# Two transformer blocks on one core: where the norm sums are added, one root for two norms, and where table loads, modulation products and row starts lie

## The reference

```python
def rms_norm(x, gain):                 # _rmsnorm of the first block is the same
    y = x * rsqrt(mean(x * x, axis=-1) + 1e-6)
    return y * gain

def first_block(x, ...):
    x = x + moba(rms_norm(x, norm_mix), w_qkv, w_o)        # 16 heads, causal softmax
    u = causal_dwconv(rms_norm(x, norm_ffn) @ w_up, ...)   # 3 taps, 2 x 2816 columns
    x = x + (silu(gate) * up) @ w_down                     # gate, up: halves of u
    return rms_norm(x, norm_final)

def second_block(x, c, ...):
    sh1, sc1, ga1, sh2, sc2, ga2, sh3, sc3, ga3 = split(silu(c) @ w_mod + b_mod, 9)
    h = rms_norm(x, g_ffn1) * (1 + sc1) + sh1
    x = x + 0.5 * (1 + ga1) * swiglu(h, w1_gate, w1_up, w1_down)
    h = rms_norm(x, g_mix) * (1 + sc2) + sh2
    x = x + (1 + ga2) * hybrid_mixer(h, ...)   # 8 stick-breaking and 8 forgetting heads
    h = rms_norm(x, g_ffn2) * (1 + sc3) + sh3
    return x + 0.5 * (1 + ga3) * swiglu(h, w2_gate, w2_up, w2_down)
```

## Time and profile before

| | us |
|---|---|
| median of 3 runs | 902.32 |
| lowest and highest | 896.45, 907.48 |
| the profiled execution | 906.59 |
| its span, first to last instruction | 904.9 |
| PE busy | 874.3 |
| DVE busy | 668.9 |
| ACT busy | 484.6 |
| POOL busy | 57.4 |

### The profile page before, as it was taken

The page is one execution under the profiler, slowest core; times in us unless marked ns, Lnnn a source line. Parts: engine busy times, 40 slices in busy tenths (PEclk is TensorE's granted clock), DMA queues, the critical chain, the costliest instruction groups (busy, mean ns, idle before and its releaser), DMA issues.

```text
span 904.9 us, 17152 instructions
## 1 busy us (share of the span) xinstructions
PE 874.3 (97%) x6920; PEld 834.2 (92%) x6920; DVE 668.9 (74%) x1396; ACT 484.6 (54%) x1008; POOL 57.4 (6%) x99
## 2 busy tenths in 40 slices
PE   6999998999999998999999998999999999999998
PEld 5888887999999997999999998878878999999998
DVE  6676657989888997998889986555643898877551
ACT  6644434777666465555555455534533665555440
POOL 4000002000000131000000026000000100000000
PEclk9999999999999999999999999979979999999999
DMA  9765356665655997767679996133004577555640
GB/s 291 251 196 179 102 190 219 209 206 192 210 187 162 337 340 278 236 231 247 227 238 317 320 343 189 47 94 95 34 13 140 186 252 240 185 187 175 204 157 25
DMA packets 151071, 179.47 MB, mean 198 GB/s; under 512 B 5712, under 2 KB 141136, under 8 KB 150992
## 3 DMA queue, kind: packets, MB, share of 16 engines
q1 hardware_dynamic: 149536, 177.65, 59.2%
q10 hardware_dynamic: 432, 0.68, 0.2%
q0 software_dynamic: 1024, 0.03, 0.1%
HBM read 177.27 MB, written 1.05 MB: 197 GB/s over the span
## 4 chain that ended last, share of the span: by engine, by line
PE 83%; DVE 10%; ACT 4%; issue 1%; DMA 1%; POOL 0%; SPq 0%; DVEq 0%; POOLq 0%
PE bank L1149 24%; PE bank L1150 24%; PE bank L1151 24%; DVE wlo L834 4%; DVE mring L905 3%; PE bank L1190 3%; PE bank L1237 1%; PE bank L1202 1%; PE bank L1194 1%; PE bank L1181 1%; PE bank L1239 1%; PE bank L1238 1%; DMA raw<-in_moba_w_qkv 1%; PE bank L1193 1%; ACT Ahi L653 1%
## 5 line engine op out<-in xcount | busy, mean ns | idle before, releaser
L1149 PE MATMUL bank<-Ahi,whi 128*128 128x258 f32 (+2 forms) x1448 | 419.8, 290 | 17.5 <-DVE wlo L834 9.0
L1150 PE MATMUL bank<-Alo,whi 128*128 128x258 f32 (+2 forms) x1448 | 411.7, 284 | 0.0
L1151 PE MATMUL bank<-Ahi,wlo 128*128 128x258 f32 (+2 forms) x1448 | 411.4, 284 | 0.0
L834 DVE TENSOR_TENSOR wlo<-raw,whi 128x512 fp32r<-128x512 f32 x528 | 352.0, 705 | 47.3 <-ACT whi L633 46.2
L633 ACT ACTIVATE whi<-raw 128x512 fp32r<-128x512 f32 x528 | 302.6, 620 | 92.6 <-PE bank L1151 77.9
L1149 PEld LDWEIGHTS bank<-Ahi,whi 128*128 128x128 f32 (+1 forms) x1448 | 277.4, 192 | 22.1 <-issue 12.0
L1150 PEld LDWEIGHTS bank<-Alo,whi 128*128 128x128 f32 (+1 forms) x1448 | 277.7, 192 | 1.1 <-issue 1.0
L1151 PEld LDWEIGHTS bank<-Ahi,wlo 128*128 128x128 f32 (+1 forms) x1448 | 276.9, 191 | 0.0
L1149 PE MATMUL bank<-Hhi,whi 128*128 128x256 f32 x528 | 147.5, 279 | 0.0
L1150 PE MATMUL bank<-Hlo,whi 128*128 128x256 f32 x528 | 147.5, 279 | 0.0
L1151 PE MATMUL bank<-Hhi,wlo 128*128 128x256 f32 x528 | 147.5, 279 | 0.0
(11 more groups left out here) (142 smaller groups left out, 797.9 us busy)
## 6 DMA issues: line engine op xcount, KB each, us to landing
mring<-in_w_mod SPq DMA_DIRECT2D x72, 512.0 KB, 6.2
raw<-in_ffn_w_up SPq DMA_DIRECT2D x22, 1024.0 KB, 5.1
raw<-in_w_gate SPq DMA_DIRECT2D x22, 1024.0 KB, 5.2
raw<-in_w_up SPq DMA_DIRECT2D x22, 1024.0 KB, 5.3
raw<-in_w_down SPq DMA_DIRECT2D x16, 1024.0 KB, 5.7
raw<-in_w_in SPq DMA_DIRECT2D x12, 1024.0 KB, 5.5
raw<-in_moba_w_qkv SPq DMA_DIRECT2D x11, 1024.0 KB, 6.7
raw<-in_ffn_w_down SPq DMA_DIRECT2D x8, 1024.0 KB, 5.8
```

Source lines behind the costliest of these rows:

```text
L834: dve.tensor_tensor(lo, raw[:, i % RAW, k0:k1, 0:width], hi.bitcast(F32), ALU.subtract).then_inc(s_wlo, 1)
L1149: pe.matmul(o, hi, xh, start=kg == 0, stop=False)
L1150: pe.matmul(o, hi, xl, start=False, stop=False)
L1151: ins = pe.matmul(o, lo, xh, start=False, stop=last and kt == nk - 1)
```

## The change

1. **Row pitch.** Ahi and Alo become flat buffers. `tiles_of` cuts them in rows of 258 floats for up2, qkv3 and up4, and in rows of 256 (1024 bytes) for qkv1 and up1.
2. **Norm sums.** ACT squares two tiles in one instruction of 512 elements: the first pair straight into `acc`, now 2 x 2 x 256, later pairs into `sq`, one pair long. DVE adds the pair to `acc` in one instruction of 512. POOL adds nothing. TensorE sums two halves of `acc` for each norm, so two fp32 matmuls where there was one, with 1/1024 in the matrix in place of a scale on ACT.
3. **One root for two norms.** With m1 the mean of x^2 and m2 that of (g x)^2, both norms together scale by 1/sqrt(m2 + eps (m1 + eps)). The second squares of up2 are taken with `fcol` = sqrt(g^2 + eps), computed once early in qkv1 (`norm_columns`, on DVE and ACT), so one Ln with bias eps^2 and one Exp give the common factor; norm_final's own factor follows with another pair. The DVE products are gone.
4. **Table loads.** `exp_ln` is called at the first squares of a norm, and `silu`, now a load of its own, right behind the root of up1, up2 and up4.
5. **Modulation products.** Still 72, at other slabs.
6. **A one-column matmul** at the first k tile of each down phase, fp32, into a column of the norm bank that nobody reads.
7. `spread_f` waits for the last chunk of down2 before it fills FA and FB, which share their place with Hhi and Hlo. `lnb` and `fcol` move ahead of Hhi.

```diff
 MOD_STEPS = {
-    "qkv1": ..., "o1": lambda i: 1 + int(i == 16), "up1": lambda i: int(i == 30),
-    "down1": lambda i: 2 - i % 2, "up2": lambda i: int(i > 54) * (i % 2 + int(i % 16 == 8)), "down2": lambda i: 2 - i % 2,
+    "qkv1": ..., "o1": lambda i: 1 + int(i == 12) - int(i == 17), "up1": lambda i: int(i == 30),
+    "down1": lambda i: 2 * int(i < 47), "up2": lambda i: int(i > 56) * (i % 2 + int(i % 8 == 0)),
+    "down2": lambda i: 2 * int(i < 85),
...
+        def tiles_of(flat, ph):
+            row = SA if ph in SHIFTED else S
+            return flat[:, 0:KD * row].rearrange("p (k c) -> p k c", c=row)
...
             def spread_f():
+                last = plan.first_of["qkv3"] - 1
+                pool.wait_ge(s_chunk, plan.chunk_done[last, slabs[last][4] // 2 - 1])
...
+            def squares(ph, q):
+                if q == 0:
+                    exp_ln()
...
+                for j in range(2 if ph == "up2" else 1):
+                    if q == 0:
+                        need.wait_ge(s_sums, NORMS.index(ph))
+                        o = acc[:, j, :, :]
+                    else:
+                        need.wait_ge(s_acc, acc_index["up1", 2, 0] if ph == "up1" and q == 3 else acc_index[ph, q, j] - 1)
+                        o = sq[:, :, :]
...
+                    elif j == 0:
+                        act.activation(o, XT[:, 2 * q:2 * q + 2, :], ACT.Square).then_inc(s_sq, 1)
...
+            def root(o, src, e):
+                need.wait_ge(s_root, ln[0])
+                act.activation(lnb[:, :], src, ACT.Ln, bias=epsc[:, e:e + 1]).then_inc(s_ln, 1)
+                ln[0] += 1
+                need.wait_ge(s_ln, ln[0])
+                act.activation(o, lnb[:, :], ACT.Exp, scale=-0.5).then_inc(s_root, 1)
+
+            def norm(ph):
...
+                if ph == "up2":
+                    root(Rr[:, 0, :], b[:, S:2 * S], 1)
+                    root(Rr[:, 1, :], b[:, 0:S], 0)
                 else:
+                    root(Rr[:, 0, :], b[:, 0:S], 0)
+                if ph in ("up1", "up2", "up4"):
+                    silu()
...
+            def add_squares(ph, q):
+                if q == 0 or (ph == "up1" and q == 3):
                     return
+                for j in range(2 if ph == "up2" else 1):
+                    need.wait_ge(s_sq, sq_index[ph, q, j])
+                    need.wait_ge(s_acc, acc_index[ph, q, j] - 1)
+                    dve.tensor_tensor(acc[:, j, :, :], acc[:, j, :, :], sq[:, :, :], ALU.add).then_inc(s_acc, 1)
...
             def multiply(i, kt):
...
+                if tag == "down" and i == plan.first_of[ph] and kt == 0:
+                    pe.matmul(banks[NORM_BANK][:, 511:512], meanf[:, :], meanf[:, 0:1], start=True, stop=True)
```

More of the change, by code:

```diff
@@ L159, in lay @@
                 lower()
-                for m in (n - 1, n):
-                    st.put("sq", "qkv1", m, 0)
+                st.put("sq", "qkv1", n // 2)
         offer(1)
@@ L279, in evict @@
                     to = NEXT_NORM[ph]
-                    for n in (c0 // P, c0 // P + 1):
-                        if to != "up1":
+                    if to != "up1":
+                        for n in (c0 // P, c0 // P + 1):
                             st.put("ain", to, n)
-                        for j in range(2 if to == "up2" else 1):
-                            st.put("sq", to, n, j)
+                    st.put("sq", to, c0 // C)
         done = 0
@@ L378, in build_program @@
         XT = sb("XT", [P, KD, S])
[L379 to L380 removed]
+        Ahi_flat = sb("Ahi", [P, KD * SA], F32R)
+        Alo_flat = sb("Alo", [P, KD * SA], F32R)
         with ExitStack() as scope:
@@ L411, in build_program @@
         bcol = sb("bcol", [P, 4])
-        epsc = sb("epsc", [P, 1])
+        epsc = sb("epsc", [P, 2])
+        lnb = sb("lnb", [P, S])
+        fcol = sb("fcol", [P, 8])
         rs = sb("rs", [P, 4, 4])
@@ L460, in build_program @@
         stick = {n: k + 1 for k, n in enumerate(m for m, h in enumerate(heads) if h[0] == "sb")}
[L461 to L464, removed]
+        sq_parts = [(s[1], s[2], j) for s in st.list if s[0] == "sq" for j in range(2 if s[1] == "up2" else 1)]
+        sq_index = {part: k + 1 for k, part in enumerate(sq_parts)}
+        acc_index = {part: k + 1 for k, part in enumerate(p for p in sq_parts if p[1] > 0 and p != ("up1", 3, 0))}
         conv_g = {g: k for k, g in enumerate(g for g, x in enumerate(groups) if x[1] in ("cg", "cu"))}
@@ L473, in build_program @@
         SHIFTED = {"up2": 1, "qkv3": 2, "up4": 3}
-        R_OF = {"qkv1": 1, "up1": 2, "up2": 3, "qkv3": 5, "up4": 6}
+        ROOT_OF = {"qkv1": 1, "up1": 2, "up2": 3, "qkv3": 5, "up4": 6}
         SHIFT_OF = {"up2": (0, 1, "g_ffn1_2"), "qkv3": (3, 4, "g_mix_2"), "up4": (6, 7, "g_ffn2_2")}
@@ new lines, in norm_columns @@
+            def norm_columns():
+                need.wait_ge(s_fcol0, 1)
+                need.wait_ge(s_eps, 2)
+                exp_ln()
+                act.activation(fcol[:, :], fcol[:, :], ACT.Ln, bias=epsc[:, 0:1]).then_inc(s_fcol0, 1)
+                need.wait_ge(s_fcol0, 2)
+                act.activation(fcol[:, :], fcol[:, :], ACT.Exp, scale=0.5).then_inc(s_fcol, 1)
+            def root(o, src, e):
[4 more added lines that the diff above has]
+                act.activation(o, lnb[:, :], ACT.Exp, scale=-0.5).then_inc(s_root, 1)
```

150 lines of the change are left out of this document (64 added, 86 removed).

## The result

| | before | after |
|---|---|---|
| median of the runs shown, us | 904.43 (4 runs) | 914.34 (4 runs) |
| ratio after to before | | 1.0115 (95% interval 1.0069 to 1.0161) |
| profiled execution, us | 906.59 | 914.62 |
| its span, us | 904.9 | 912.4 |

The account below looks back on a forecast made before the run. TensorE, busy for 97% of the span, was taken as the bound. Terms summed to 16.9 us saved; 902.3 - 16.9 + 1.3 (a half-clock stretch) gave 886.7 us, range 878 to 899.

Parts of the forecast that it names:

- Row pitch, -5.8 and -1.5: 1024-byte rows of Ahi and Alo take up1 to the fast 113.1 ns pace, saving 5.8 us, and save 1.5 in qkv1.
- Rival 1: up1 settles at the slow aligned pace and keeps what it enters with: gain 4.7 us less, 891.4 us; chance 0.23.
- One-column matmul, -4.1: An fp32 matmul ahead puts down2 and down4 on the fast pace: 4.9 us saved, less 0.8 for three matmuls.
- rival 2: Columns alone set the pace; differences come from another source, such as what the weights' tiles meet: 898.9 us; chance 0.13.
- The gap rule: Start-to-start gap from column count alone, 109 ns for 256 columns; by it pitch and extra matmul would change nothing.
- Modulation products, +0.5: Two products per slab in down1 and down2 leave VectorE 1 to 3 us late at down2's end, costing 0.5 us.
- rival 4: Starved of products: down2 loses 9 us, down1 8, up2's 3.4 gain goes; 907 us; decides past two slabs (10 us) late; chance 0.05.
- GpSimd, -0.7 at the start and -0.3 in o3: Its 46 adds and copies go, VectorE is slowed less: 0.7 us saved at the start, 0.3 in o3.
- The entry of up2: Of 4.4 us of TensorE waits between 343.9 and 360.7, 3.4 us go, net of four more norm passes.
- The root of qkv3: At qkv3's entry the table load moves to down2's first squares: 0.9 us saved, net of two norm passes.
- the 1.3 us at half clock: At qkv3's entry the clock may hold after an idle cut to some 1.9 us, saving 1.3 us more.
- The entry of up1: Last residual starts about 1.2 us sooner, but copies of Ahi wait for a 1.28 us silu load: 0.3 us saved.

Follow-up runs that it names:

- the mixed version: Kernel after with lnb and fcol behind W8, no silu load behind up1's root, products as before in down2, none in down1's last two slabs: 896.0 us, ratio 0.989.
- The timed version: The mixed version with Ahi and Alo moved to Hhi's place and one-column matmuls ahead of up1's second and sixth slab: 892.4 us, ratio 0.9844 to the kernel before.

## Why the prediction was wrong

**Row pitch, -5.8 and -1.5.** Wrong: +1.3 in up1, 0.0 in qkv1. The step that failed is "there are two settled paces for aligned rows", with Hhi's rows taken as the model for Ahi's. The runs show that it counts where the moving tile stands to the weights' tiles modulo 128 bytes. The pitch only makes every row stand alike. Hhi stood well, 64 past; Ahi stood at 0, Alo at 64, and up1 settled at 117.8 or 120.0. With Ahi moved to 64 as well, the forecast's 113 came in a part of up1 (four slabs, then thirteen), and qkv1 won 3.5 ns. Rival 1 had the pace kept through the phase right, and its size wrong.

**One-column matmul, -4.1.** Its mechanism was right: with Hhi's place put back, 117.8 became 113.4 in down2 and down4. In the profiles with Hhi at that place (counted from the weights, modulo 1024 bytes) 22 of 24 down phases behind it ran at 113.4, and 3 of 9 without it. Its price of 0.8 us for three was about right: in the timeline of after it takes 0.14 us, and the first matmul behind it 0.20 instead of 0.12, in all 0.22 each:

```profile
285.86 0.28 PE L1173 MATMUL bank<-meanf 128*128 128x1 f32 x2
286.00 0.36 PE L1179 MATMUL bank<-Hhi,whi 128*128 128x256 f32 x1
286.20 0.28 PE L1180 MATMUL bank<-Hlo,whi 128*128 128x256 f32 x1
```

But the 1056 bytes under Hhi took the gain and more: down1 +2.6 us (528 x 4.9 ns), down2 and down4 +0.3 each, o1 +0.6. These bytes stood in the prediction, as an argument inside rival 2 ("if their place mattered it would show as a slower down1"), with no price of their own. That sign came, and the edit belonged in the sum. (In the sum of down1 and up2 the loss is smaller than in down1, as the run with 32 bytes shows.)

**The gap rule.** The Trainium skill ("TensorE: Matmul & The Clock Gate", section "Back-to-back issue gap") has the formula by columns alone that gives 109 ns, but calls it the gap of an isolated matmul. For a stream of weight loads and matmuls, which this kernel is, it says that both set the spacing, and gives about 81 ns at 128 columns, about 131 at 512 and nothing for 256. So the prediction held the formula against a case for which the section gives other figures. In the runs 256 columns settled at 113.3, 117.8, 118.3 and 120.0 ns, by place, and none reached 109. So columns alone don't set the pace here, and that part of rival 2 falls; its other part, that the differences come from what the tiles meet, was nearest to what the runs show.

**Modulation products, +0.5.** This is the step that turned the sign in qkv3: "Up to three weight slabs and three products are loaded ahead, and that cover is worth some 5 us in each queue, so I expect VectorE 1 to 3 us late". It was 8.9 us late. The three buffers were counted as cover, but the queue is in order: with two products in each slab, SyncE stands on a buffer that VectorE has yet to free while VectorE stands on one that has yet to land. The cost, a wait of 7.8 us in qkv3 and 1.5 us of waits in down1, is rival 4, though neither by its bandwidth (355 GB/s went through with a fourth buffer) nor at the place where it was priced. Its point of decision, VectorE two slabs late, was nearly reached.

**GpSimd, -0.7 at the start and -0.3 in o3.** At the start nothing was saved: the wait of 0.98 us is gone, but the first matmul came 0.3 us later and the granted clock was full from 14.4 us on instead of 14.0. O3 got 0.8 us shorter at a pace 4.3 ns slower; no run took GpSimd's share apart.

**What was right.** The entry of up2: -3.4 forecast, -3.8 measured; no wait left. Here some luck helped. A down1 slowed by 32 bytes alone gave up2 2.7 us in the kernel before, and the products alone gave 2.9. With down1 at 113.4 ns and the products where they were, the rest of the change gave 1.6 us (up2 130.4), or nothing without the one-column matmul (132.1, 3.4 us of it at half clock); in the mixed version it came to 3.3 (128.7). So about half of the gain or more came from the products that left the end of down1, and in after down1's loss of 4.1 us outweighs it. The root of qkv3: 0.9 us forecast, 1.3 measured (2.8 to 1.5), though the late residual hid it. Once the products are put back, qkv3's entry holds the full clock, but so did the kernel before with 32 bytes more, behind the same wait of 2.8 us (granted 1.00 from 545 to 553 us). So the 1.3 us at half clock were not shown to hang on the length of the wait. The entry of up1: -0.3 forecast, -0.1 measured, from a product that left (-1.1, by the run with the products put back) against a load that came (+0.75, by the mixed version without it); the rest, 0.2, is not explained. Here the Trainium skill ("ScalarE: Activation LUTs", section "What ACT_TABLE_LOAD costs") with 2.66 us per switch would have given a loss; the load took 1.28 us and the next activation began 0.01 us behind it, so the row held again. Up4's two norm passes: +0.45 as priced.

## What to carry to other kernels

A new small tensor is an edit to every tile allocated behind it: before pricing anything else, work out what the addresses of the matmuls' moving tiles become to the weights' tiles, and try the change with the tensor at the end. A prefetch ring that is refilled in order by the queue that also loads the weights must be held against the burst, not the mean: n buffers cover n products only while neither side waits for the other. Where a phase changes pace for good, look for the short wait at which it changed.

## What the runs showed that was not expected

*Place and pace.* Matmuls of 128x256 at the full clock, with the moving tiles' place against the weights' modulo 128 bytes: at 64, 113.3 or 117.8 ns; at 96, 118.3; at 0, 120.0 mostly (118.7 in one down4); one tile at 0 and one at 64, 117.8 or 120.0. Once settled, a pace changed in no profile of up1 and the down phases without a wait or hitch of TensorE between, the shortest of 0.07 us; behind one it is drawn anew and can come out the same. Open: in the run with rows of 1088 bytes Hhi and Hlo also stood at 64, yet all three down phases took 117.8 in spite of the one-column matmul; with rows of 1152 bytes two of three did. At least that draw depends on more than the place modulo 128.

*Scatter.* The timed version ran from 884.4 to 897.3 us in six runs, and the kernel before from 895.8 to 908.9 beside it. The profiles differ most in o3. The window of o3 with everything moved by 64 bytes, and in the last version:

```profile
660.00:694.00 34.00, 33.23 (x257) 29.68 (x258) 21.94 (x55) 17.83 (x44) 0.00 (x0) 1.00 0.42 135
```

```profile
660.00:702.00 42.00, 41.56 (x259) 36.18 (x258) 22.18 (x55) 18.13 (x44) 0.00 (x0) 0.78 0.35 111
```

The same work takes 33.0 and 40.8 us, at a granted clock of 1.00 and 0.78. From qkv3's last matmul to o3's first 3.0 us passed in the slower one and 1.8 in the other; but in the slower one the clock had fallen 2.4 us ahead of qkv3's last matmul, so the longer gap didn't start it. That is more than most edits here are worth, and no run settled what decides it.
